# Splitting the second expert's weights too, and handing the mixture-of-experts' preparation round between ScalarE, VectorE and GpSimd

## What is computed

```python
def hier_moe(h, w_rg, b_rg, w_re, b_re, w_g, w_u, w_d):
    ...
    hid = jax.nn.silu(jnp.einsum('bsd,edf->bsef', h, w_g)) * jnp.einsum('bsd,edf->bsef', h, w_u)
    hid = hid * gate[..., None].astype(hid.dtype)
    return jnp.einsum('bsef,efd->bsd', hid, w_d)
```

## Time and profile before

| | us |
|---|---|
| median of 3 runs | 1389.27 |
| the 3 runs | 1387.70, 1389.38, 1389.27 |
| the profiled execution | 1387.39 |
| its span, first to last instruction | 1385.6 |

### The profile page before, as it was taken

How to read it: one execution, slowest core, us unless ns; L and a number is a source line. 1 busy time by engine, 2 the same in 40 slices (tenths; PEclk the granted TensorE clock), 3 DMA queues, 4 the chain that set the end, 5 groups by cost and what they waited for, 6 DMA issues and landing times.

```text
span 1385.6 us, 19946 instructions
## 1 busy us (share of the span) xinstructions
PE 1351.8 (98%) x6972; PEld 1046.3 (76%) x6972; DVE 892.1 (64%) x2057; ACT 580.0 (42%) x1238; POOL 761.6 (55%) x603
## 2 busy tenths in 40 slices
PE   7999999999999999999789999999999999999997
PEld 5788877777777876777577888777777778677774
DVE  4487866646684347988446787665566741588882
ACT  4323334343433135676343432434334321466761
POOL 4566654454345664567555576455444457546673
PEclk9999999999999999999989999999999999999999
DMA  5436422223222569999632242222223128699993
GB/s 155 131 93 175 128 71 87 62 78 105 84 67 67 203 269 349 354 371 369 135 116 76 61 137 78 79 77 72 83 90 90 62 76 291 238 368 365 357 345 87
DMA packets 115066, 225.35 MB, mean 163 GB/s; under 512 B 18666, under 2 KB 28324, under 8 KB 114958
## 3 DMA queue, kind: packets, MB, share of 16 engines
q1 hardware_dynamic: 102526, 198.64, 42.6%
q0 software_dynamic: 9936, 16.81, 5.3%
q10 hardware_dynamic: 2496, 8.52, 1.6%
HBM read 216.52 MB, written 31.25 MB: 179 GB/s over the span
## 4 chain that ended last, share of the span: by engine, by line
PE 92%; DVE 4%; POOL 1%; issue 1%; ACT 1%; DMA 1%; POOLq 0%; SPq 0%; DVEq 0%; ACTq 0%
PE bank L987 23%; PE bank L989 22%; PE bank L988 22%; PE bank L1284 5%; PE bank L1163 4%; PE bank L1175 3%; PE bank L1196 2%; PE bank L1244 2%; PE bank L1116 1%; PE bank L1186 1%; POOL w_lo L842 1%; PE bank L1129 1%; DVE probs L2003 1%; DVE mixed L1820 1%; PE bank L1254 1%
## 5 line engine op out<-in xcount | busy, mean ns | idle before, releaser
L836 POOL TENSOR_SCALAR w_hi<-raw 128x1024 fp32r<-128x1024 f32 (+2 forms) x142 | 149.8, 1055 | 409.3 <-PE bank L989 406.6
L842 POOL TENSOR_TENSOR w_lo<-raw,w_hi 128x512 fp32r<-128x512 f32 (+2 forms) x288 | 359.4, 1269 | 16.4 <-ACT w_hi L1732 4.6
L988 PE MATMUL bank<-w_hi,hT_lo 128*128 128x512 f32 (+2 forms) x696 | 258.7, 372 | 0.0
L987 PE MATMUL bank<-w_lo,hT_hi 128*128 128x512 f32 (+2 forms) x576 | 216.8, 376 | 2.0 <-DVE hT_lo L1828 1.0
L989 PE MATMUL bank<-w_hi,hT_hi 128*128 128x512 f32 (+2 forms) x576 | 211.7, 368 | 0.0
L987 PE MATMUL bank<-hT_lo,w_hi 128*128 128x512 f32 x384 | 159.4, 415 | 0.0
L989 PE MATMUL bank<-hT_hi,w_hi 128*128 128x512 f32 x384 | 150.7, 392 | 0.0
L988 PE MATMUL bank<-hT_hi,w_lo 128*128 128x512 f32 x384 | 150.2, 391 | 0.0
L988 PEld LDWEIGHTS bank<-w_hi,hT_lo 128*128 128x128 f32 x696 | 131.5, 189 | 20.2
L987 PEld LDWEIGHTS bank<-w_lo,hT_hi 128*128 128x128 f32 x576 | 108.7, 189 | 28.0 <-issue 8.5
L989 PEld LDWEIGHTS bank<-w_hi,hT_hi 128*128 128x128 f32 x576 | 108.6, 188 | 17.9
(11 more groups left out here) (359 smaller groups left out, 2836.5 us busy)
## 6 DMA issues: line engine op xcount, KB each, us to landing
raw<-in_w_gate SPq DMA_DIRECT2D x48, 512.0 KB, 3.8
work<-in_w_ff_gate SPq DMA_DIRECT2D x46, 512.0 KB, 6.5
work<-in_w_ff_up SPq DMA_DIRECT2D x46, 512.0 KB, 8.7
work<-in_w_ff_down SPq DMA_DIRECT2D x23, 1024.0 KB, 8.6
raw<-in_w_in SPq DMA_DIRECT2D x40, 512.0 KB, 3.6
raw<-in_w_branch SPq DMA_DIRECT2D x24, 512.0 KB, 3.6
w_lo_raw<-in_w_ff_down SPq DMA_DIRECT2D x10, 1024.0 KB, 8.1
X<-in_w_ff_gate SPq DMA_DIRECT2D x20, 512.0 KB, 5.8
```

The costliest lines, as they stand in the source:

```text
L836: nc.gpsimd.tensor_scalar(w_hi[:, two, :, 0:w], raw[:, slot, :, 0:w], 1.0, 0.0, ALU.mult, ALU.add).then_inc(split_hi, 1)
L842: last = nc.gpsimd.tensor_tensor(w_lo[:, two, kk, 0:w], raw[:, slot, kk, 0:w], w_hi[:, two, kk, 0:w].bitcast(F32), ALU.subtract)
L987: nc.tensor.matmul(out_ap, s_hi, m_lo, start=start, stop=False)
L988: nc.tensor.matmul(out_ap, s_lo, m_hi, start=False, stop=False)
```

## The change

`FIRST_SPLIT` goes from 2 to 1, so that expert 1 is split like those after it. The high and low parts of gate and up are made per piece, not per pair of K-tiles: two instructions for an expert, 128 x 1024 for piece 0 (K-tiles 2 and 3) and 128 x 2048 for piece 1, where there were three of 128 x 1024. Expert 0's down weights get their high parts from GpSimd and their low parts from VectorE. The high part of the hidden rows goes from VectorE to ScalarE (`hidden_hi`). The order on ScalarE and VectorE within an iteration is new: VectorE subtracts piece 1 of expert e + 1 and piece 0 of expert e + 2 in iteration e, ahead of the hidden rows' low part and of its half of the result. `route_blocks` moves from iterations 2 and 3 to 3 and 5, and what TensorE does with its tables from 5 and 6 to 7 and 8. Semaphores are renamed.

```diff
-FIRST_SPLIT, SPLIT_FROM = 2, 2
-SPLIT_PAIRS = (8 - SPLIT_FROM) // 2
+FIRST_SPLIT, SPLIT_FROM = 1, 2
...
-        gu_hi_bufs = [[oT_hi[:, 0:2], oT_hi[:, 2:4], oT_lo[:, 0:2], oT_lo[:, 2:4]],
-                      [hT_lo[:, 0:2], hT_lo[:, 2:4], hT_hi[:, 4:6], hT_hi[:, 6:8]]]
+        gu_hi_bufs = [[oT_hi[:, 0:4], oT_lo[:, 0:4]], [hT_lo[:, 0:4], hT_hi[:, 4:8]]]
...
+                def first_weights_hi():
+                    pool.wait_ge(arrived(0, 2), loaded(0, 2))
+                    for c in range(2):
+                        nc.gpsimd.tensor_scalar(w_hi[:, c, :, :], down_rows(0)[:, :, c * 512:(c + 1) * 512], 1.0, 0.0,
+                                                ALU.mult, ALU.add).then_inc(down_hi, 1)
...
-                weights_lo(0)
+                first_weights_hi()
...
-                        if (kt - SPLIT_FROM) % 2 == 0:
-                            pe.wait_ge(gu_lo, split_pairs(e - 1) + pair + 1)
+                        if kk == first:
+                            pe.wait_ge(gu_lo, split_parts(e - 1) + part + 1)
...
+            def gate_up_hi(e, part):
+
+                first = 0 if part else SPLIT_FROM
+                act.wait_ge(arrived(e, part), loaded(e, part))
+                nc.scalar.activation(high_of(e, part), gate_up_piece(e, part)[:, :, first:4, :], ACT.Copy).then_inc(gu_hi, 1)
...
             def weights_hi(e):
                 act.wait_ge(arrived(e, 2), loaded(e, 2))
+                if e == 1:
+                    act.wait_ge(down_lo, 2)
...
+            def hidden_hi(e):
+                act.wait_ge(hid_turned, e + 1)
+                if e >= 2:
+                    act.wait_ge(down_done, 2 * (e - 1))
+                nc.scalar.activation(hid_hi[:, e % 2, :], T[e % 2][:, 0:FF], ACT.Copy).then_inc(hidT_hi, 1)
...
-                weights_hi(0)
+                act.wait_ge(logits_done, 2)
+                gate_up_hi(1, 0)
+                gate_up_hi(1, 1)
                 et_out(0)
...
+                    if splits(e + 2):
+                        gate_up_hi(e + 2, 0)
+                    if 1 <= e < N_EXPERTS - 1:
+                        weights_hi(e)
                     if e >= 1:
                         rows_down(e - 1)
+                    if e < N_EXPERTS - 1:
+                        hidden_hi(e)
...
-                    if 1 <= e < N_EXPERTS - 1:
-                        weights_hi(e)
                     if splits(e + 2):
-                        gate_up_hi(e + 2)
+                        gate_up_hi(e + 2, 1)
...
             def experts():
+                gate_up_lo(1, 0)
                 et_out(0)
+                gate_up_lo(1, 1)
                 route_rest()
...
+                    if splits(e + 1) and e:
+                        gate_up_lo(e + 1, 1)
+                    if e == 0:
+                        hidden_lo(e)
+                        route_over()
+                        for c in range(2):
+                            v.wait_ge(down_hi, c + 1)
+                            nc.vector.tensor_tensor(down_low(0)[:, :, c * 512:(c + 1) * 512],
+                                                    down_rows(0)[:, :, c * 512:(c + 1) * 512],
+                                                    w_hi[:, c, :, :].bitcast(F32), ALU.subtract).then_inc(down_lo, 1)
+                    if splits(e + 2):
+                        gate_up_lo(e + 2, 0)
+                    if 1 <= e < N_EXPERTS - 1:
+                        down_lo_half(e)
...
+                    elif 1 <= e < N_EXPERTS:
+                        hidden_lo(e)
+                    if e >= 1:
+                        rows_right(e - 1)
                     if e == 1:
                         route_rows()
...
-                    if e in (2, 3):
-                        route_blocks(e - 2)
-                    if e == 5:
+                    if e in (3, 5):
+                        route_blocks((3, 5).index(e))
+                    if e == 7:
```

More of the change, by code:

```diff
@@ L383, in first_native, with high_of @@
             return SPLIT_FROM if splits(e) else KT
-        def pair_hi_of(e, kt):
-            return gu_hi_bufs[e % 2][(kt - SPLIT_FROM) // 2]
+        def high_of(e, part):
+            first = 0 if part else SPLIT_FROM
+            return (gu_hi_bufs[e % 2][part].rearrange("p k n -> p (k n)")[:, 0:512 * (4 - first)]
+                    .rearrange("p (h k n) -> p h k n", h=2, n=FF))
         def tiles_of(slot_rows):
@@ L918, in weights_lo @@
                     rows = down_rows(e)
[L919 to L925, removed]
+                    pool.wait_ge(down_hi, 2 * e + 1)
+                    for f in range(2):
+                        last = nc.gpsimd.tensor_tensor(down_low(e)[:, f, 0:512], rows[:, f, 0:512],
+                                                       w_hi[:, 0, f, :].bitcast(F32), ALU.subtract)
+                    last.then_inc(down_lo, 1)
+                def first_weights_hi():
[3 more added lines that the diff above has]
+                                                ALU.mult, ALU.add).then_inc(down_hi, 1)
                 def rows_added(b):
@@ L934, in add_last_rows @@
                     pool.wait_ge(y_out[l][e % 4], 16 * (e // 4))
-                    for c, ready in enumerate((y_act, y_dve)):
+                    for c, ready in enumerate((y_left, y_right)):
                         pool.wait_ge(ready, e + 1)
@@ L1286, in gate_up @@
                     else:
-                        pair = (kt - SPLIT_FROM) // 2
+                        first = 0 if part else SPLIT_FROM
                         if kt == SPLIT_FROM:
                             pe.wait_ge(et_dve, e + 1)
-                        if (kt - SPLIT_FROM) % 2 == 0:
-                            pe.wait_ge(gu_lo, split_pairs(e - 1) + pair + 1)
+                        if kk == first:
+                            pe.wait_ge(gu_lo, split_parts(e - 1) + part + 1)
                         last = three(G[e % 2][:, :], et_hi[:, e % 2, rows], et_lo[:, e % 2, rows],
-                                     pair_hi_of(e, kt)[:, (kt - SPLIT_FROM) % 2, :], gate_up_low(e, part)[:, :, kk, :],
+                                     high_of(e, part)[:, :, kk - first, :], gate_up_low(e, part)[:, :, kk, :],
                                      kt == 0, kt == KT - 1)
@@ L2271, in et_out, with gate_up_lo @@
                                         ALU.subtract).then_inc(et_dve, 1)
[L2273 to L2280 removed]
+            def gate_up_lo(e, part):
+                first = 0 if part else SPLIT_FROM
+                v.wait_ge(gu_hi, split_parts(e - 1) + part + 1)
+                nc.vector.tensor_tensor(gate_up_low(e, part)[:, :, first:4, :], gate_up_piece(e, part)[:, :, first:4, :],
+                                        high_of(e, part).bitcast(F32), ALU.subtract).then_inc(gu_lo, 1)
             def down_lo_half(e):
```

84 lines of the change are left out of this document (30 added, 54 removed).

## The result

| | before | with the change |
|---|---|---|
| median (lowest to highest, runs) | 1388.49 (1387.27 to 1389.38, 4) | 1397.20 (1396.55 to 1398.04, 4) |
| the profiled execution | 1387.39 | 1397.15 |
| its span | 1385.6 | 1395.3 |
| TensorE's granted clock, mean over the span | 0.994 | 0.991 |

Ratio 1.0064, with a 95% interval of 1.0049 to 1.0079: 8.7 us slower, where 1395.5 us had been forecast with a range of 1390.5 to 1401.5. Between the profiled executions it is 9.7 us of span.

The account below looks back on a forecast made before the run. TensorE was taken to set the pace in the expert stage, with VectorE next in line. Terms of +3.8 (queue), +2.4 and +0.9 (VectorE's list) summed to +7.1 us on 1388.5, predicting 1395.5 us, range 1390.5 to 1401.5.

Parts of the forecast that it names:

- Part 1: Splitting expert 1 takes 1.04 us of TensorE's work out of each layer; by itself worth -0.9 us a layer.
- Part 2: On ScalarE hidden_hi(0) stands behind the copy awaiting expert 2's pieces, delaying route_over and L1410: +1.70 and +2.06, together +3.8 us.
- the steps: Landing to L1410: copy 0.95, hidden_hi 0.38, hand-over 0.13, hidden_lo 0.34, route_over 3.22, hand-over 0.08; 5.10 us.
- Part 3: VectorE's list, 9.4 us an expert; route_rows makes TensorE wait 1.2 us at down(2) per layer, 2.4; route_blocks adds 0.9.
- The turns: VectorE's subtractions alternate with GpSimd's halves, instruction by instruction; two GpSimd halves of 1.24 us each enter VectorE's chain per expert.
- Part 4: Expert 0's low parts, wider ScalarE copies, later overflow tables and later result rows to DRAM: all put at nothing.
- The sum: +3.8 + 2.4 + 0.9 = +7.1 us for the whole kernel; 1395.5 us predicted.
- Rival 1: VectorE's next subtraction precedes GpSimd's waiting half; its chain is 2.5 us shorter, never late: +3.8, 1392.3 us; chance 0.20.
- rival 3: VectorE's chain reaches 10.1 us; TensorE waits 0.35 us in some 12 iterations per layer, 8.4 more: 1403.9 us; chance 0.15.
- Rival 2: Expert 2's pieces land 2.6 us earlier (3.0 in the second layer), the w_ready wait vanishes: 1386.6 us; chance 0.10.

Follow-up runs that it names:

- the run with native weights: Changed kernel with expert 0's hidden copy ahead of the copy that waits for expert 2's piece, and expert 1's gate and up native: 1389.85 us, ratio 1.0012.
- The busy wait: Changed kernel plus 12 matmuls whose result is never read, on TensorE ahead of its wait for route_over: 1393.04 us, ratio 1.0032.
- the last experiment: Changed kernel with expert 0's hidden copy first, plus one unused 128x1024 VectorE subtraction for each of experts 5 to 15: 1400.30 us, ratio 1.0085.
- the repaired order: Changed kernel with ScalarE copying expert 0's hidden rows ahead of the copy that waits for expert 2's piece 0: 1386.16 us, again 1386.83 us.

## Why the prediction was right, and where its reasons were not

**Part 1, the split of expert 1: right.** gate_up(1) starts at 529.11 (529.3 forecast), its last product at 534.72, and by 535.1 TensorE is idle. The gain is swallowed by the wait. Its size, 1.04 us a layer, was a little low: 1.13 from gate_up(1) to L1410 in the run with native weights.

**Part 2, the queue: right in mechanism and in size.** L1410 was forecast for 537.83 and starts at 537.86; the second layer's shift of its own was forecast at 2.06 and is 2.07. The runs show the queue as the cause: without it the wait is gone, put into the kernel before it makes the wait, and in the four kernels with the queue that were read so L1410 starts 5.13 to 5.15 us behind the landing in both layers, where the steps had been added up to 5.10. The forecast idle time of 2.6 us is 2.75 and 3.12.

**A term was missing: what the wait does to TensorE's clock.** The step that failed is the end of part 2, where TensorE "only waits longer" and the sum takes +3.8 for it. The wait is followed by 1.67 and 3.31 us lost at half clock, 5.0 us together, which is more than the wait. The busy wait shows it: it removes the slow stretches and 4 us of the time. The trace of before gave a warning. In the stretch that answers to the two slow ones the clock is 1.00, but at the boundary between the layers, behind the 9.5 us that TensorE idles ahead of L1012, the kernel before has

```profile
697.00:699.00 2.00, 2.00 (x11) 0.50 0.64 168
```

with TensorE busy for all of it. So that kernel too ran slowly for a while behind a long wait. That a wait of 2.6 us is enough could not be read from it, but the forecast did not even have it in its bounds. The Trainium skill, page "TensorE: Matmul & The Clock Gate", section "Part 1: The HAM clock gate (the "warmup" mystery)", says that the clock drops to half behind idling and that in three kernels measured there its ratio took two values only. The traces here agree: 0.50 and 1.00, with mixed values where a stretch takes in a change.

**Part 3, VectorE's list: the mechanism was right, the term mis-sized, +3.3 against 0.** Two things made it nothing. VectorE's own chain is 0.5 us an expert shorter than worked out. The turns cost it 1.1 us each (575.84 to 578.08 less 1.14), not GpSimd's 1.24 from start to start, and piece 1, the hidden rows' low part and the right half come to 2.20, 0.33 and 0.66 us where 2.3, 0.4 and 0.7 had been put. And TensorE, held up by its clock, came to `down(2)` late itself: at 561.50, when the hidden rows' low part, started at 560.12, was done. With the queue in place and the clock kept full the stall does appear, at its forecast place, iteration 2 of the first layer. VectorE in the kernel with the busy wait, and then TensorE:

```profile
555.61 2.32 DVE L2290 TENSOR_TENSOR work_low<-work,oT_hi 128x1024 fp32r<-128x1024 f32 x1
557.85 2.31 DVE L2296 TENSOR_TENSOR w_lo<-w_lo_raw,w_hi 128x1024 fp32r<-128x1024 f32 x1
560.09 0.41 DVE L2302 TENSOR_TENSOR hT_lo<-bank,hT_lo 128x256 fp32r<-128x256 f32 x1
```

```profile
559.54 1.04 PE L1244 MATMUL bank<-ident,probs 128*128 128x128 f32 x8
560.55 0.50 PE L987 MATMUL bank<-w_lo,hT_lo 128*128 128x512 f32 x1
```

The transposes need 0.80 us to the next start when nothing holds (551.04 to 551.84 in the changed kernel), here 1.01: 0.2 us of stall, not 1.2, and none in the second layer. Without the queue there is none at all. For `route_blocks` the forecast had 0.9; in the changed kernel the iterations behind it take 9.7 us like the others, and it costs TensorE something (1.71 and 1.52 us in the first layer) only in the last experiment, where VectorE has nothing to spare.

**Part 4: wrong in one clause.** "Result rows go to DRAM later in an iteration; they are waited for only four experts on" holds for the slots of an expert, not for the last ones: behind expert 15 the next layer waits for all of them. The wide copies, expert 0's low parts and the overflow tables did cost nothing: without the queue TensorE has no idle time there, and an expert takes what it took. This clause cost 1.4 us.

**The sum** was therefore right for partly wrong reasons: 3.8 as forecast, 5.0 + 1.5 - 0.6 where it had 3.3. Only the wait was foreseen, 3.8 of 9.7 us; that terms which were not forecast took the place of one that came out at nothing is luck, and without the clock's fall and the loss between the layers the forecast would have been too high. Rival 1 (VectorE keeps the port) falls by the turns in the last experiment, although its outcome, a VectorE that is never late, is what the changed kernel has; rival 3 (VectorE the bound throughout) needs 0.8 us more an expert, as that experiment shows by adding 1.14 and getting 0.3. Rival 2's number, 1386.6, is what the repaired order reaches (1386.2 and 1386.8), by a shorter queue rather than by an earlier landing, which did not happen.

**What stays open:** why 1.40 us of idling brought the clock down and 1.71 did not; why the clock then stays low for 3.4 us in some cases and 6.8 in others; and why the last addition takes 0.76 us longer to land, which is half of the loss between the layers.

## What to carry to other kernels

An instruction that everybody wants must not stand behind one that waits for a transfer: look at who is behind each wait of an engine's list, above all in the first round, where the transfers are late. A wait that stops TensorE for some microseconds is to be priced with what the slow stretch behind it can cost, here up to 3.3 us and more than the wait itself, and a dozen matmuls of no use in such a wait can pay. When an instruction is moved later "because nobody needs it yet", look at the last iteration on its own.

## What the runs showed of the hardware

- TensorE's granted clock halved behind idle times of 2.75 and 3.12 us in the changed kernel, and behind 1.40, 1.87, 2.62 and 3.11 us in three others; it stayed full behind 0.44 and 1.71 us, and behind the four waits of 1.5 to 1.7 us of the kernel with more work for VectorE. In these cases it did not fall during the wait (in the 9.5 us between the layers of the kernel before it was at half by 690, 6 us ahead of L1012), but when TensorE was working again: in the changed kernel 1.9 us after L1410 had started in the first layer (537.86, 539.8) and 0.2 us after it in the second (1225.63, 1225.9). It stayed low for 3.4 us (four cases) or 6.8 us (two), which cost 1.7 or 3.3 us; the longer idle time did not have the longer low stretch (2.62 us had 6.8, 3.11 us had 3.4).
- VectorE's subtractions with both inputs in SBUF and GpSimd's alternate instruction by instruction: one of 128x1024 takes 1.22 us by itself and about 2.3 us when a half of GpSimd's goes first.
- From gate_up(2) to L1321 TensorE took 137.58 to 137.60 us in eight profiled executions of the changed kernel and its variants, on several chips, but the medians of one and the same kernel before lay 0.5 us apart between chips (1388.14, 1388.61, 1388.18); a difference of 1 us needs both kernels on one chip.
